# The expert stage's gather reads its moving operand in steps of eight columns, and the transposes behind it read contiguous blocks

## The reference

```python
def hier_moe(t, w_group, b_group, w_expert, b_expert, w_gate, w_up, w_down):
    ...
    gates = jnp.sum(w_sel[..., None] * jax.nn.one_hot(expert_id, N_EXPERTS, dtype=jnp.float32), axis=1)
    ...
    for e in range(N_EXPERTS):
        hid = jax.nn.silu(t @ w_gate[e]) * (t @ w_up[e])
        y = y + gates[:, e:e + 1] * (hid @ w_down[e])
    return y
```

## Time and profile before

| | |
|---|---|
| median of 3 runs | 935.59 us (932.93 to 940.14) |
| the profiled execution: its own time | 937.84 us |
| its span in the profile | 936.0 us |
| TensorE matmul (PE): busy | 910.9 us, 97% |
| TensorE weight load (PEld): busy | 553.2 us, 59% |
| VectorE (DVE): busy | 405.2 us, 43% |
| ScalarE (ACT): busy | 310.1 us, 33% |

### The profile page before, as it was taken

The page is one execution under the profiler, slowest core; times in us unless marked ns, Lnnn a source line. Parts: engine busy times, 40 slices in busy tenths (PEclk is TensorE's granted clock), DMA queues, the critical chain, the costliest instruction groups (busy, mean ns, idle before and its releaser), DMA issues.

```text
span 936.0 us, 11843 instructions
## 1 busy us (share of the span) xinstructions
PE 910.9 (97%) x4576; PEld 553.2 (59%) x4576; DVE 405.2 (43%) x836; ACT 310.1 (33%) x648; POOL 156.3 (17%) x220
## 2 busy tenths in 40 slices
PE   8999999999999999999999999999999999999996
PEld 6877766787443344443677777777884344443433
DVE  6667557435132233324568554464434233223123
ACT  5544558624111111112445445464342111101110
POOL 3433323310000000000311445441010000000000
PEclk9999979999999999999999999999999999999999
DMA  9835532378999999999444363444978999999994
GB/s 301 280 132 192 170 142 57 141 270 346 361 423 423 421 423 421 416 419 413 165 132 128 129 190 116 141 136 154 396 288 326 405 423 421 424 420 423 421 423 171
DMA packets 56654, 271.04 MB, mean 290 GB/s; under 512 B 5842, under 2 KB 6082, under 8 KB 32019
## 3 DMA queue, kind: packets, MB, share of 16 engines
q1 hardware_dynamic: 47698, 242.14, 65.5%
q0 software_dynamic: 8896, 28.09, 9.2%
HBM read 260.44 MB, written 9.77 MB: 289 GB/s over the span
## 4 chain that ended last, share of the span: by engine, by line
PE 86%; DVE 5%; DMA 4%; ACT 2%; issue 1%; POOL 1%; SPq 0%; ACTq 0%; DVEq 0%; POOLq 0%
PE ps L1627 22%; PE ps L1645 11%; PE ps L1154 7%; PE ps L1156 7%; PE ps L1155 7%; DMA w_extra<-in_moe_w_up 3%; PE ps L1659 2%; PE ps L1212 2%; PE ps L1213 2%; PE ps L1660 2%; PE ps L1408 2%; PE ps L1412 2%; PE ps L1605 1%; PE ps L1315 1%; PE ps L1312 1%; PE ps L1586 1%
## 5 line engine op out<-in xcount | busy, mean ns | idle before, releaser
L1627 PE MATMUL ps<-w_extra,xT 128*64 128x512 f32 x512 | 162.5, 594 | 0.0
L1627 PE MATMUL ps<-w_raw,xT 128*64 128x512 f32 x320 | 141.7, 593 | 1.3 <-DMA w_extra<-in_moe_w_up 1.3
L1154 PE MATMUL ps<-w_hi,hT_hi 128*128 128x512 f32 x224 | 93.9, 419 | 0.5 <-DVE gate L1982 0.3
L1752 DVE TENSOR_TENSOR w_lo<-w_raw,w_hi 128x2048 fp32r<-128x2048 f32 x31 | 70.6, 2287 | 48.9 <-ACT w_hi L796 48.9
L1156 PE MATMUL ps<-w_hi,hT_lo 128*128 128x512 f32 x224 | 88.4, 395 | 0.0
L1155 PE MATMUL ps<-w_lo,hT_hi 128*128 128x512 f32 x224 | 88.4, 395 | 0.0
L1627 PEld LDWEIGHTS ps<-w_raw,xT 128*64 128x64 f32 x320 | 43.2, 137 | 72.6 <-issue 72.6
L1627 PE MATMUL ps<-w_more,xT 128*64 128x512 f32 x192 | 85.3, 594 | 0.3 <-DMA w_extra<-in_moe_w_up 0.3
L1645 PE MATMUL ps<-w_extra,hidT 128*64 128x512 f32 x240 | 82.8, 596 | 0.5 <-ACT hidT L1120 0.5
L1627 PEld LDWEIGHTS ps<-w_extra,xT 128*64 128x64 f32 x512 | 50.1, 137 | 49.5 <-issue 49.3
L1645 PE MATMUL ps<-w_raw,hidT 128*64 128x512 f32 x168 | 75.7, 597 | 0.0
(11 more groups left out here) (313 smaller groups left out, 1635.6 us busy)
## 6 DMA issues: line engine op xcount, KB each, us to landing
w_extra<-in_moe_w_up SPq DMA_DIRECT2D x35, 1024.0 KB, 16.8
w_extra<-in_moe_w_down SPq DMA_DIRECT2D x30, 1024.0 KB, 17.8
w_extra<-in_moe_w_gate SPq DMA_DIRECT2D x29, 1024.0 KB, 15.9
w_raw<-in_moe_w_gate SPq DMA_DIRECT2D x25, 1024.0 KB, 17.0
w_raw<-in_moe_w_down SPq DMA_DIRECT2D x21, 1024.0 KB, 16.2
w_raw<-in_fox_w_in SPq DMA_DIRECT2D x16, 1024.0 KB, 5.6
w_raw<-in_moe_w_up SPq DMA_DIRECT2D x15, 1024.0 KB, 13.1
w_more<-in_moe_w_up SPq DMA_DIRECT2D x14, 1024.0 KB, 20.9
```

Source lines behind the costliest of these rows:

```text
L1154: mm(out, a_hi, b_hi, start=start, stop=False)
L1627: ins = mm(ps[j * CAP:(j + 1) * CAP, bank, :], xT[:, kb, j * CAP:(j + 1) * CAP], buffer(U.slot)[:, k * F:(k + 1) * F], start=(kb == 0), st ...
L1752: v.tensor_tensor(w_lo[:, U.slot, :], w_raw[:, U.slot, :], w_hi[:, U.hslot, :].bitcast(F32), ALU.subtract).then_inc(lo_ready, 1)
```

## The change

`gather` reads the moving operand in steps of eight columns, in an order in which value 8q + 4c + k of a token comes to column 128k + q of half c. So half c of PSUM, and of `x_slots`, holds the four blocks 4c to 4c + 3, each in 128 contiguous columns. For gathered pairs `transpose_slots` takes these blocks, and its wait for the second copy moves behind the first four transposes, which read the first half alone. Pairs that are fetched by rows keep both the layout and the stepped transposes. The number of matmuls, copies and transposes stays the same.

```diff
+                def by_block(rows, t, c):
+                    return rows[:, t, :].rearrange("p (q k) -> p k q", k=KB)[:, 4 * c:4 * c + 4, :]
+
                 def gather(i):
...
-                            mm(ps[:, 5 + c, :], pick[:, t, cols], h2_hi[:, t, c * F:(c + 1) * F], start=(t == order[0]), stop=False)
+                            mm(ps[:, 5 + c, :], pick[:, t, cols], by_block(h2_hi, t, c), start=(t == order[0]), stop=False)
...
-                                ins = mm(ps[:, 5 + c, :], pick[:, t, cols], h2_lo[:, t, c * F:(c + 1) * F], start=False, stop=(t == order[-1]))
+                                ins = mm(ps[:, 5 + c, :], pick[:, t, cols], by_block(h2_lo, t, c), start=False, stop=(t == order[-1]))
...
                         pe.wait_ge(L["slots_act"], B["slots_act"] + on_pe(l, i) + 1)
-                        pe.wait_ge(L["slots_dve"], B["slots_dve"] + on_pe(l, i) + 1)
                     for c in range(2):
+                        if c == 1 and i not in BY_ROWS[l]:
+                            pe.wait_ge(L["slots_dve"], B["slots_dve"] + on_pe(l, i) + 1)
                         for k in range(4):
-                            ins = tr(ps[:, 5 + c, k * P:(k + 1) * P], every(x_slots[:, :], 4 * c + k, KB), ident)
+                            block = every(x_slots[:, :], 4 * c + k, KB) if i in BY_ROWS[l] else x_slots[:, (4 * c + k) * P:(4 * c + k + 1) * P]
+                            ins = tr(ps[:, 5 + c, k * P:(k + 1) * P], block, ident)
```

## The result

The changed kernel takes 952.78 us (median of 4 runs, 950.97 to 954.47), the kernel before, run beside it, 936.09 us. The ratio is 1.0198, with an interval of 1.0172 to 1.0225: slower by 16 to 21 us. A second comparison, 6 runs beside 17 of before, gave 949.33 against 933.63 us, a ratio of 1.0131 (1.0095 to 1.0168). These ratios are as recorded; the quotients of the medians are 1.0178 and 1.0168, or 16.7 and 15.7 us. The forecast was 949.4 us and 1.5%. So the sign and most of the size came out, the first measurement lies 3.4 us above the forecast, and the intervals of the two comparisons of one and the same pair of kernels do not meet. Both differences want an answer.

A forecast was written before the change was run, and what follows sets the result against it. TensorE's queue was taken to bound the kernel, except 1.7 us of weight waits in layer 1. 9.9 + 4.0 + 1.6 - 1.7 = 13.8 us, added to the median 935.59, gave 949.4 us (1.5% slower); range 934 to 954.

The forecast's parts named there:

- Value taken: 0: Layer heads: transposes moved under the second copy gain nothing, as slots(0) waits 0.40 us for pick_gate; at most 1.2 us.
- The price: Ninety gather matmuls with a moving operand in steps of eight: 0.198 us more each, half pace; chance 0.62.
- the upper end: Gather matmuls: stepped loads at 193 ns against 141 ns imply half pace; 0.198 us taken for each matmul.
- The lower end: Gather matmuls: price 0, since eight stepped transposes go at the same pace as eight contiguous ones.
- The reason given beside the price: Moving read of the gather: steps of eight fp32 are 32 bytes, so every column is in a new 16-byte line.
- layer 0's gathers: Five gathers in layer 0's loop, each 2.0 us longer on TensorE's queue: +9.9 us.
- the heads: First gather matmul to first "gate" in each layer: longer gather, partly offset by early transposes; +0.8 us each, +1.6 us.
- layer 1's last stretch: Layer 1's two looped gathers, +4.0 us, less 1.7 us of waiting that comes back: +2.3 us.
- the wait that comes back: Last pair of layer 1: TensorE arrives later and no longer waits for its last weights: -1.7 us.
- The read that keeps its pace: Rival, ninety gather matmuls: price 0 to 0.02 us each, total 0 to -0.5 us, 935.4 us; chance 0.25.
- the price of two passes: Rival, gather matmuls: 0.626 us more each, as two f32 passes; +51.6 us, 987 us; chance 0.06.
- early transposes that pay: Rival, layer heads: gain of at most 1.2 us, 934.4 us, only if pick_gate were ready sooner; chance 0.02.

The follow-up runs named there:

- rows_in_blocks: Against the kernel before: VectorE writes h2 in block order, reading x and gain in steps of eight; gather and transposes read contiguous columns; ratio 0.9987.
- the fours: Against the kernel before: all gathers read four contiguous columns in every eight, with early transposes kept; ratio 1.0009.
- pairs: Against the kernel before: all gathers read two contiguous columns in every eight, with early transposes kept; ratio 1.0165.

## Why the prediction came out as it did

*The gain.* "Value taken: 0", because slots(0) waits for pick_gate. Right in its mechanism: wherever the gather kept its pace, the time saved on the copy went into the wait for pick_gate (rows_in_blocks; in the fours the two waits for it are 1.7 us).

*The price.* Right: 0.200 us measured, 0.198 taken. The choice of the upper end, by the stepped loads at 193 ns, held. The objection that 193 ns might be the ordinary pace of a load falls: on one line the 72 gathered loads went to some 140 ns, the others stayed. And the loads care as little how wide the step is: in the runs with moving steps of two and of four, where the gathered transposes read x_slots in steps of four and of two, the 128 loads take 202 and 201 ns in the mean. The lower end was no test of a moving read: in a stepped transpose the identity moves, and the step is in the load.

*The reason given beside the price.* Half right. The Trainium skill's page "SBUF — State Buffer" ("Door 1: The DMA port swizzle", on cachelines) has it that fp32 can be stepped over for free up to four elements, and that a 16-byte line wants at least two hits to be read at full bandwidth. For the steps of eight it pointed the right way. The runs disagree with it on smaller ones, for this moving operand: steps of two and of four, and pairs, all go at half pace, 0.45 to 0.46 us, and only four contiguous columns at 0.23 us. The measurement decides.

*The sum.* Right where it was made: 13.93 us measured in the four stretches, 13.8 forecast; layer 0's gathers 9.83 for 9.9, the heads 2.17 for 1.6, layer 1's last stretch 1.93 for 2.3. That the total agrees so closely is partly luck, for the errors of the heads (+0.57) and of the last stretch (-0.37) offset each other. At the head the sum put the hand-overs from engine to engine at nothing: in layer 0 the second copy ends at 228.95 and the transposes start at 229.01, the copy of xT ends at 230.30 and "gate" starts at 230.40. In the last stretch the wait that comes back was worth 2.09 us, not 1.7: the last pair's stretch between the transposes of hid shrank from 26.72 to 24.63 us. The starts around the two waits, in the kernel before, show why:

```profile
905.49 0.59 PE L1627 MATMUL ps<-w_more,xT 128*64 128x512 f32 x1
906.43 0.61 PE L1627 MATMUL ps<-w_more,xT 128*64 128x512 f32 x1 [0.34 <-DMA w_extra<-in_moe_w_up]
...
909.49 0.59 PE L1627 MATMUL ps<-w_extra,xT 128*64 128x512 f32 x1
911.39 0.61 PE L1627 MATMUL ps<-w_raw,xT 128*64 128x512 f32 x1 [1.31 <-DMA w_extra<-in_moe_w_up]
```

They are 0.94 and 1.90 us apart where the step is 0.43, so 1.98 us are lost. The waits add up to 1.65 only, since the profile counts a wait from the end of a matmul, 0.59 us after its start.

*What failed* is the step ahead of the sum, "the granted clock is 1.00, so TensorE runs at its upper level, 2.4 GHz, throughout", and with it the range. The clock was read in the expert pairs only. It falls elsewhere: over the whole span of the very execution that was read its mean was 0.990, and from 117 to 133 us it was 0.68. In the first execution after, layer 1's router took 4.37 us more at a clock of 0.73. Time at the lower level is a term that the sum put at nothing, and the runs of one and the same kernel spread by 8 us with it (932.10 to 940.38). By the 0.43 us of above it made some 8 us in the changed kernel's first four runs, 4 us in its next six, and 5 us in the 17 of before. That is about 3 us of the first comparison's 16.7, if its four runs of before, whose clocks are not on record but for one, lost as much as the 17. The range allowed 2 us for spread above its dearest price. In microseconds 952.78 still lies below its upper end of 954; the recorded ratio, 1.0198, lies just beyond (954 us are 1.0197 times the 935.59 that the forecast was added to), and the second, 1.0131, within. On which side of the end a comparison falls is the chance of the clock in its runs.

*The rivals.* The read that keeps its pace and the price of two passes are excluded by the 0.431 us; early transposes that pay, by the head of the kernel with blocks but no stepped gather, 5.57 us as before. In the second of them 70 times 0.626 is 43.8 us, not 43.9; nothing hangs on it.

## What to carry to other kernels

Here a float32r matmul kept its pace (0.23 us) with its moving operand in runs of four contiguous columns, each beginning at a multiple of 16 bytes, and fell to half of it with runs of one or two; if an order has to be changed, change it in fours, or on an engine with idle time. Before a wait is shortened, look which wait ends next behind it: here it was 0.4 us away, and took everything. And where runs of one kernel spread by more than the effect, compare them at the same granted clock, and stretch by stretch at the same marks.

## What the runs showed that was not expected

- Steps of two columns are as slow as steps of eight (0.451 and 0.431 us for 512 columns), and pairs too (0.463); fours are not (0.233).
- VectorE pays for steps as well: the norm of 128 x 1024 values with steps of eight in both inputs took 2299 ns, contiguous 1284 ns. It lies ahead of the router: layer 1's router stretch grew from 14.70 to 15.27 us, both at a clock of 1.00, too little to show in the total (0.9987).
- The granted clock falls in the same few places, but not in each of them in every run, nor for as long. In the fourteen profiled executions it falls between 206 and 223 us and at the very end each time, between 117 and 133 us in nine, in layer 1's router in eight. In the changed kernel's two, that router stood at 0.73 and at 1.00 over the same instructions, its small matmuls and the filling ones between them; in the fours, whose gather is as fast as before, the stretch from 680 to 720 us stood at 0.87.
